# A decoder layer on one core: Relu and square of the up pairs as one pass on VectorE in place of two on ScalarE

## The chip, the cores and the metric
The kernel runs on one core of one Trainium2 chip. The metric is the device time of one execution, in microseconds (us). The engines are TensorE (PE; its weight loads are PEld), VectorE (DVE), ScalarE (ACT), GpSimd (POOL) and SyncE (SP), each with an instruction queue of its own that it works through in order. They wait for each other through semaphores.

## What is computed
One decoder layer on x of 512 x 1024, float32: RMSNorm, one input projection, latent attention and sparse attention, an output projection, then the part that matters here, a squared-ReLU MLP with 4096 hidden columns.

```
h2 = rms_norm(x, ln2_g[l])
x = x + jnp.square(jax.nn.relu(h2 @ w_up[l])) @ w_down[l]
```

## The kernel before
Products are made in float32 accuracy from halves: each factor is split into `hi` (ScalarE copies it, rounded) and `lo` (VectorE subtracts `hi` from the factor), and a product is three matmuls, hi x hi, lo x hi and hi x lo. Weights come in pieces of 128 x 1024 through a ring of three `raw` tiles, are split into a ring of five `w_hi` / `w_lo` tiles, and are used from there. `split_hi(n)` and `split_lo(n)` make the halves of piece n. SyncE loads a piece into `raw` when the tile's last reader has signalled (`lo_done`, for some pieces the subtraction `w_diff` as well).

The hidden columns are 32 chunks of 128; all outputs lie in `a_all` (32 x 512 in the free dimension). The first 4 chunks are done singly (ScalarE's Relu and Square, lines 1286 on, not touched here). The other 28 are done as 14 pairs (PAIRS = 14) with fewer block products, by sums and differences of blocks as in Strassen's method. For pair p:
- TensorE: `sum_products(p)` (24 matmuls of 256 columns from piece A, then 12 called D), `own_products(p + 1)` (24, piece P), `last_products(p)` (24, piece B): 84 a pair. `last_products(p)` waits for `cross_out(p)`. In the last round (p = 13) `job(0)` stands in the place of `own_products`.
- ScalarE: `keep(p)` copies the sum bank to SBUF once A is done.
- VectorE: `cross_out(p)` (line 1848) adds bank and kept sum into the two cross quarters of the pair's output, `first_out(p)` (1856, 1857) updates the kept sum, `diagonal_out(p)` (1864) writes the two diagonal quarters with the sign turned, once B is done. It also makes the weight differences (`diff_of`, `diff_lo`; ScalarE's `diff_hi` between them) and every second pair `row_diffs(i)` (1869, 1870).
- ScalarE then runs, in place on each half of the output (128 x 512), Relu (line 1249, scale 1 on the cross, -1 on the diagonal quarters) and Square (1251). `cross_square(p)` stands behind `keep(p)`, and `diagonal_square(p)` in the next round ahead of `keep(p + 1)`; for the last pair it stands behind `job_hi(3)`.

The down projection is 56 jobs (`JOBS`) of 12 matmuls of 512 columns, 8 steps of 4 and then 8 of 3. Job d needs two splits: `job_hi(d)` on ScalarE (its factor, line 1298, then its weights, 1307) and `job_lo(d)` on VectorE (`factor_lo_of`, 1927, then `weight_lo_of`, 1935; for an m5 job `weight_difference`, 1913, ahead of them). The factors of m1, m2 and m5 are differences that VectorE makes in `factor_of` (1949) from quadrants of the squared `a_all`. Jobs 0 to 3 are m2, m5, m3, m1 of step 0, jobs 4 and 5 are m2 and m5 of step 1. At the seam the order in the queues is written out by hand. VectorE: round 12 ends with `factor_of` m1 and m2 of step 0 and `job_lo(0)`; round 13 is `diagonal_out(12)`, `factor_of("m5", 0)`, `weight_difference(0)`, `factor_lo_of(1)`, `cross_out(13)`, `first_out(13)`; then `weight_lo_of(1)`, `job_lo(2)`, `job_lo(3)`, `diagonal_out(13)`, `factor_of` m1, m2, m5 of step 1, `job_lo(4)`, `job_lo(5)` and so on. ScalarE: `diagonal_square(12)`, `job_hi(1)`, `keep(13)`, `cross_square(13)`, `job_hi(2)`, `job_hi(3)`, `diagonal_square(13)`, `job_hi(4)`.

Of the kernel before, what the change touches and what calls it, by code (L numbers as in the profile page):

```python
# [22 lines left out]
ALU = mybir.AluOpType  # L23
ACT = mybir.ActivationFunctionType
# [37 lines left out]
STARTED = 4  # L62
PAIRS = (N_UP - STARTED) // 2
# [3 lines left out]
JOBS = [(m, i) for i in range(STEPS) for m in (GROUP_A if i < STEPS - 1 else ("m2", "m5", "m1", "m3"))]  # L67
# [257 lines left out]
def build(nc, a, out, known):  # L325
    with ExitStack() as ctx:
# [14 lines left out]
        def signal(name, step=1):  # L341
            return Signal(nc, ctx, name, known, step)
# [119 lines left out]
        def s_halves(d):  # L462
            return s_all[:, d % S_RING, 0, :, :], s_all[:, d % S_RING, 1, :, :]
# [29 lines left out]
        def pair_slots(p):  # L493
            return a_all[:, STARTED + 2 * p:STARTED + 2 * p + 2, :].rearrange("p f (h s) -> p (f h) s", h=2)

        def cross(p):
            return pair_slots(p)[:, 1:3, :]

        def diagonal(p):
            return pair_slots(p)[:, 0::3, :]  # L500

        def pair_sum(p):
            return s_tmp[2 + p % 2]
# [61 lines left out]
        dve_step, x2_done, sq_done, factor_lo = signal("dve_step"), signal("x2_done"), signal("sq_done"), signal("factor_lo")  # L565
        part_in, factor_diff, job_used = signal("part_in"), signal("factor_diff"), signal("job_used")
        rows_kept, g_kept, g_sum, g_hi, g_lo, uv_done = signal("rows_kept"), signal("g_kept"), signal("g_sum"), signal("g_hi"), signal("g_lo"), signal("uv_done")
        weight_diff, pair_kept, pair_out, pair_relu = signal("weight_diff"), signal("pair_kept"), signal("pair_out"), signal("pair_relu")
        y_done = signal("y_done")

        rsqrt_done, pool_step, roped = signal("rsqrt_done"), signal("pool_step"), signal("roped")
# [63 lines left out]
        def pair_banks(p):  # L635

            x_, z_ = (D, S)[p % 2]
            return x_, z_, T[p % 2][:, 0:2 * P]
# [283 lines left out]
        def _(act):  # L922
# [321 lines left out]
                n = PIECE_AT["P", p]  # L1244
                act.activation(d_halves[p % 2][0], raw[:, n % RAW, 0:512], ACT.Copy).then_inc(*hi_done.mark(("d", p)))

            def squared(key, tile, scale):

                act.activation(tile, tile, ACT.Relu, scale=scale).then_inc(*pair_relu.mark(key))
                act.wait_ge(*pair_relu.at(key))  # L1250
                act.activation(tile, tile, ACT.Square).then_inc(*sq_done.mark(key))

            def keep(p):

                if p >= 2:
                    act.wait_ge(*pair_out.at(("diagonal", p - 2)))
                act.wait_ge(*dense_done.at(("A", p)))
                act.activation(pair_sum(p), pair_banks(p)[1].rearrange("p (h s) -> p h s", h=2), ACT.Copy).then_inc(*pair_kept.mark(p))

            def cross_square(p):  # L1260
                act.wait_ge(*pair_out.at(("cross", p)))
                squared(("cross", p), cross(p), 1.0)

            def diagonal_square(p):
                act.wait_ge(*pair_out.at(("diagonal", p)))
                squared(("diagonal", p), diagonal(p), -1.0)

            ln_his(1, [0])
            to_hi(("mix", 1, 0), act_hi[:, 4:8, 0:P], 4, P)
# [11 lines left out]
            for f in range(STARTED):  # L1281
                key = ("up", f)
# [10 lines left out]
            def job_hi(d):  # L1293

                m, i = JOBS[d]
                act.wait_ge(*job_factor_free(d))
                act.wait_ge(*(factor_diff if m in DIFF_OF else uv_done).at(JOBS[d] if m in DIFF_OF else i))
                act.activation(s_halves(d)[0], factor(d), ACT.Copy).then_inc(*factor_hi.mark(JOBS[d]))
                act.wait_ge(*job_slot_free(d))
                if m == "m1":  # L1300
                    act.wait_ge(*dve_step.at(("w_diff", i)))
                    src = w_diff
                else:
                    n = job_piece(d)
                    act.wait_ge(*raw_in[n % RAW].at(n))
                    src = quads(raw[:, n % RAW, :])
                act.activation(job_halves(d)[0], src, ACT.Copy).then_inc(*hi_done.mark(JOBS[d]))  # L1307

            for p in range(PAIRS):
                if p + 2 < PAIRS:  # L1310
                    split_hi(PIECE_AT["P", p + 2])
                if p:
                    diagonal_square(p - 1)
                if p == PAIRS - 1:
                    job_hi(1)
                if p == PAIRS - 2:
                    split_hi(PIECE_AT["B", p + 1])
                keep(p)
                cross_square(p)
                if p + 2 < PAIRS:  # L1320
                    diff_hi(p + 2)
                    split_hi(PIECE_AT["B", p + 1])
                if p + 2 < PAIRS:
                    split_hi(PIECE_AT["A", p + 2])
                if p == PAIRS - 2:
                    job_hi(0)
            job_hi(2)
            job_hi(3)
            diagonal_square(PAIRS - 1)
            for d in range(4, len(JOBS)):  # L1330
                job_hi(d)


# [1 line left out]
        def _(dve):  # L1335
            def split_lo(n):

                width, (hi, lo) = PIECES[n][2], halves_of(n)
                dve.wait_ge(*hi_done.at(n))
                if PIECES[n][0] == "wo":  # L1340
                    for j, gain in enumerate(group_gains(n)):
                        cols = slice(512 * j, 512 * j + 512)
                        ins = dve.scalar_tensor_tensor(lo[:, cols], raw[:, n % RAW, cols], gain,
                                                       hi[:, cols].bitcast(F32), ALU.mult, ALU.subtract)
                else:
                    ins = dve.tensor_tensor(lo[:, 0:width], raw[:, n % RAW, 0:width],  # L1346
                                            hi[:, 0:width].bitcast(F32), ALU.subtract)
                ins.then_inc(*lo_done.mark(n))
# [495 lines left out]
            def cross_out(p):  # L1844
# [2 lines left out]
                dve.wait_ge(*pair_kept.at(p))  # L1847
                dve.tensor_tensor(cross(p), halves(x_)[:, ::-1, :], pair_sum(p), ALU.add).then_inc(*pair_out.mark(("cross", p)))

            def first_out(p):  # L1850

                w_ = pair_banks(p)[2]
                z = pair_sum(p)
                dve.wait_ge(*dense_done.at(("D", p)))
                dve.wait_ge(*pair_out.at(("cross", p)))
                dve.tensor_tensor(z[:, 0, :], z[:, 0, :], w_, ALU.subtract)
                dve.tensor_tensor(z[:, 1, :], z[:, 1, :], w_, ALU.add).then_inc(*pair_out.mark(("first", p)))

            def diagonal_out(p):

                x_, _, _ = pair_banks(p)
                dve.wait_ge(*dense_done.at(("B", p)))
                dve.wait_ge(*pair_out.at(("first", p)))
                dve.tensor_tensor(diagonal(p), halves(x_), pair_sum(p), ALU.add).then_inc(*pair_out.mark(("diagonal", p)))

            def row_diffs(i):

                dve.wait_ge(*sq_done.at(("diagonal", 2 * i - 1) if i else STARTED - 1))
                dve.tensor_tensor(quadrant((0, 1), i), quadrant((0, 0), i), quadrant((0, 1), i), ALU.subtract)
                dve.tensor_tensor(quadrant((1, 0), i), quadrant((1, 0), i), quadrant((1, 1), i), ALU.subtract).then_inc(*uv_done.mark(i))  # L1870

# [88 lines left out]
            for p in range(PAIRS):  # L1960
                if p:
                    diagonal_out(p - 1)
                if p + 2 < PAIRS:
                    split_lo(PIECE_AT["P", p + 2])
                if p == 0:
                    factor_low("G6", 1)
                    factor_low("G6", 0)
                if p == PAIRS - 1:
                    factor_of("m5", 0)
                    weight_difference(0)  # L1970
                    factor_lo_of(1)
                cross_out(p)
                if p + 2 < PAIRS:
                    diff_of(p + 2)
                first_out(p)
                if p + 2 < PAIRS:
                    diff_lo(p + 2)
                if p + 1 < PAIRS:
                    split_lo(PIECE_AT["B", p + 1])
                if p + 2 < PAIRS:  # L1980
                    split_lo(PIECE_AT["A", p + 2])
                if p == 1:
                    row_diffs(0)
                if p and p % 2 == 0:
                    row_diffs(p // 2)
                if p == PAIRS - 2:
                    factor_of("m1", 0)
                    factor_of("m2", 0)
                    job_lo(0)
            weight_lo_of(1)  # L1990
            job_lo(2)
            job_lo(3)
            diagonal_out(PAIRS - 1)
            for m in ("m1", "m2", "m5"):
                factor_of(m, 1)
            for d in range(4, len(JOBS)):
                m, i = JOBS[d]
# [648 lines left out]
```

## Time and profile before
| | us |
|---|---|
| median of 3 runs | 650.25 (649.61 to 651.02) |
| profiled execution, its own time | 649.47 |
| its span, first to last instruction | 647.2 |
| TensorE busy | 637.0 (98%) |
| VectorE busy | 497.7 (77%) |
| ScalarE busy | 395.4 (61%) |
| GpSimd busy | 161.0 (25%) |

The granted clock of TensorE is 1.0 of full speed in every slice. Matmuls are pipelined: one is recorded with 0.28 us (256 columns) or 0.39 us (512), and the next starts 0.12 or 0.23 us behind it; some of their records are missing. So the pace of TensorE is read from start times. Instructions of VectorE and ScalarE overlap a little as well: the next one may start before the recorded end of the one ahead.

### The profile page before, as it was taken

The numbers are of one execution on the slowest core, as the hardware profiler recorded it, in microseconds if no ns is written. First come the engines' busy times: TensorE is split into PE (matmuls) and PEld (weight loads), VectorE is DVE, ScalarE is ACT, GpSimd is POOL, SyncE is SP. The second block draws the span as 40 slices with busy tenths as digits, with TensorE's granted clock in tenths as the row PEclk, the third lists the DMA queues.
The fourth block names the chain that finished last, engine by engine and source line by source line (L and its number), as shares of the span: only waits on it lengthen the run. The fifth ranks groups of instructions, "written<-read, shape, count | busy, mean of one in ns | idle before, by whom it ended". The sixth has DMA issues, their size and how long they took to land.

```text
span 647.2 us, 11797 instructions
## 1 busy us (share of the span) xinstructions
PE 637.0 (98%) x4189; PEld 566.1 (87%) x4189; DVE 497.7 (77%) x915; ACT 395.4 (61%) x784; POOL 161.0 (25%) x229
## 2 busy tenths in 40 slices
PE   8999999999999999998999999999999999999998
PEld 5999888887789888887899999999998888888886
DVE  5665746479887888897786787778768999898675
ACT  6554666467897647556447666757657655565471
POOL 1416755444332201112110111111112221222200
PEclk9999999999999999999999999999999999999999
DMA  8383538998998964896371687887877899999984
GB/s 288 121 310 131 196 129 290 303 305 217 250 269 255 356 205 164 260 268 156 65 188 67 188 236 195 216 217 194 231 177 163 188 250 221 233 237 268 265 246 158
DMA packets 33933, 140.40 MB, mean 217 GB/s; under 512 B 5097, under 2 KB 5481, under 8 KB 32915
## 3 DMA queue, kind: packets, MB, share of 16 engines
q1 hardware_dynamic: 22114, 81.63, 36.2%
q0 software_dynamic: 10208, 34.88, 29.9%
q10 hardware_dynamic: 1552, 23.14, 9.5%
q8 instruction: 34, 0.56, 0.4%
q14 instruction: 25, 0.20, 0.1%
HBM read 137.48 MB, written 65.06 MB: 313 GB/s over the span
## 4 chain that ended last, share of the span: by engine, by line
PE 93%; DVE 3%; ACT 2%; issue 1%; DMA 0%; ACTq 0%; DVEq 0%
PE bank L2052 15%; PE bank L2054 15%; PE bank L2053 15%; PE bank L2469 7%; PE bank L2470 7%; PE bank L2471 7%; PE bank L2072 7%; PE bank L2304 3%; PE bank L2247 2%; PE bank L2286 2%; PE bank L2400 2%; PE bank L2399 2%; PE bank L2401 2%; PE bank L2258 1%; PE bank L2259 1%
## 5 line engine op out<-in xcount | busy, mean ns | idle before, releaser
L841 POOL DMA_DIRECT2D down_sums<-w_down x64 | 49.8, 779 | 235.1 <-PE bank L2471 143.1
L1346 DVE TENSOR_TENSOR w_lo<-raw,w_hi 128x1024 fp32r<-128x1024 f32 (+3 forms) x70 | 80.2, 1158 | 21.8 <-ACT w_hi L938 21.5
L2052 PE MATMUL bank<-w_hi,act_hi 128*128 128x512 f32 (+3 forms) x224 | 89.8, 401 | 2.1 <-DVE act_lo L1360 0.9
L938 ACT ACTIVATE w_hi<-raw 128x1024 fp32r<-128x1024 f32 (+3 forms) x70 | 68.5, 993 | 33.6 <-DMA raw<-w_pairs 22.6
L2053 PE MATMUL bank<-w_lo,act_hi 128*128 128x512 f32 (+3 forms) x224 | 79.8, 356 | 0.0
L2054 PE MATMUL bank<-w_hi,act_lo 128*128 128x512 f32 (+3 forms) x224 | 79.8, 356 | 0.0
L1074 ACT ACTIVATE p_buf<-s_buf,stats 128x128 f32<-128x128 f32 (+3 forms) x96 | 53.8, 561 | 32.4 <-PE bank L2072 18.1
L1307 ACT ACTIVATE w_hi<-raw 128x1024 fp32r<-128x1024 f32 x31 | 32.8, 1059 | 35.9 <-DMA raw<-down_sums 16.9
L2052 PE MATMUL bank<-w_hi,s_all 128*128 128x512 f32 x140 | 54.6, 390 | 0.0
L2053 PE MATMUL bank<-w_lo,s_all 128*128 128x512 f32 x140 | 54.6, 390 | 0.0
L2054 PE MATMUL bank<-w_hi,s_all 128*128 128x512 f32 x140 | 54.5, 390 | 0.0
L2052 PEld LDWEIGHTS bank<-w_hi,act_hi 128*128 128x128 f32 x224 | 42.3, 189 | 10.1 <-issue 2.6
L2053 PEld LDWEIGHTS bank<-w_lo,act_hi 128*128 128x128 f32 x224 | 42.4, 189 | 6.1 <-issue 1.4
L2469 PE MATMUL bank<-g_all,w_hi 128*128 128x256 f32 x168 | 47.7, 284 | 0.0
L2471 PE MATMUL bank<-g_all,w_lo 128*128 128x256 f32 x168 | 47.6, 284 | 0.0
L2471 PE MATMUL bank<-act_hi,w_lo 128*128 128x256 f32 x168 | 47.6, 284 | 0.0
L2469 PE MATMUL bank<-act_hi,w_hi 128*128 128x256 f32 x168 | 47.6, 284 | 0.0
L2470 PE MATMUL bank<-act_lo,w_hi 128*128 128x256 f32 x168 | 47.6, 284 | 0.0
L2470 PE MATMUL bank<-g_all,w_hi 128*128 128x256 f32 x168 | 47.6, 283 | 0.0
L2054 PEld LDWEIGHTS bank<-w_hi,act_lo 128*128 128x128 f32 x224 | 42.2, 188 | 5.4
L1935 DVE TENSOR_TENSOR w_lo<-raw,w_hi 128x1024 fp32r<-128x1024 f32 x31 | 37.8, 1219 | 11.5 <-ACT w_hi L1307 11.4
L2072 PE MATMUL bank<-consts,p_buf 128*128 128x128 f32 x248 | 45.0, 279 | 1.6 <-ACT p_buf L1074 0.8
(313 smaller groups left out, 1830.6 us busy)
## 6 DMA issues: line engine op xcount, KB each, us to landing
down_sums<-w_down ACTq DMA_DIRECT2D x32, 512.0 KB, 6.5
down_sums<-w_down POOLq DMA_DIRECT2D x64, 256.0 KB, 5.6
raw<-down_sums SPq DMA_DIRECT2D x32, 512.0 KB, 5.4
up_sums<-w_pairs POOLq DMA_DIRECT2D x28, 512.0 KB, 10.2
raw<-up_sums SPq DMA_DIRECT2D x28, 512.0 KB, 4.9
raw<-weights SPq DMA_DIRECT2D x26, 512.0 KB, 5.8
up_sums<-w_pairs SPq DMA_DIRECT2D x16, 512.0 KB, 6.5
raw<-w_down SPq DMA_DIRECT2D x16, 512.0 KB, 5.3
```

Source lines behind the costliest of these rows:

```text
L841: pool.dma_start(sums_dram[k, rows_], a["w_down"][SUMS[m][1], step, rows_], accum_op=ALU.add, max_dma_last_dim=4096).then_inc(*sum_added[k ...
L938: ins = act.activation(hi[:, 0:width], raw[:, n % RAW, 0:width], ACT.Copy)
L1074: act.activation(p_buf[:, n % 2, 0:nk], s_buf[:, n % 2, 0:nk], ACT.Exp, scale=-1.0, bias=neg_max[:, m:m + 1], accum_out=den[:, d:d + 1]).t ...
L1346: ins = dve.tensor_tensor(lo[:, 0:width], raw[:, n % RAW, 0:width], hi[:, 0:width].bitcast(F32), ALU.subtract)
L1935: dve.tensor_tensor(lo, src, hi.bitcast(F32), ALU.subtract).then_inc(*lo_done.mark(JOBS[d]))
L2052: pe.matmul(dst, a_h, w_h, start=start, stop=False, skip_group_check=onto)
L2053: pe.matmul(dst, a_h, w_l, start=False, stop=False, skip_group_check=onto)
L2054: return pe.matmul(dst, a_l, w_h, start=False, stop=stop, skip_group_check=onto)
L2072: ins = pe.transpose(bank[0:m, i * step:i * step + k], tile, ident[0:k, 0:k])
L2469: pe.matmul(dst, h[:, k * P:(k + 1) * P], g_h[:, k, :], start=start and k == 0, stop=False, skip_group_check=onto)
L2470: pe.matmul(dst, h[:, k * P:(k + 1) * P], g_l[:, k, :], start=False, stop=False, skip_group_check=onto)
L2471: ins = pe.matmul(dst, l[:, k * P:(k + 1) * P], g_h[:, k, :], start=False, stop=k == KD // 2 - 1, skip_group_check=onto)
```

## The change
Relu and square are no longer two ACTIVATE instructions on ScalarE but one `scalar_tensor_tensor` on VectorE: (t max 0) * t on the cross quarters, (t min 0) * t on the diagonal ones, whose sign is turned. It is still in place and still 128 x 512. `keep`, `job_hi` and the others on ScalarE stay in their order without the squares; the new passes stand in VectorE's queue.

```diff
-            def squared(key, tile, scale):
-
-                act.activation(tile, tile, ACT.Relu, scale=scale).then_inc(*pair_relu.mark(key))
-                act.wait_ge(*pair_relu.at(key))
-                act.activation(tile, tile, ACT.Square).then_inc(*sq_done.mark(key))
-
...
-            def cross_square(p):
-                act.wait_ge(*pair_out.at(("cross", p)))
-                squared(("cross", p), cross(p), 1.0)
-
-            def diagonal_square(p):
-                act.wait_ge(*pair_out.at(("diagonal", p)))
-                squared(("diagonal", p), diagonal(p), -1.0)
...
             for p in range(PAIRS):
                 if p + 2 < PAIRS:
                     split_hi(PIECE_AT["P", p + 2])
-                if p:
-                    diagonal_square(p - 1)
                 if p == PAIRS - 1:
                     job_hi(1)
...
                 keep(p)
-                cross_square(p)
...
             job_hi(2)
-            job_hi(3)
-            diagonal_square(PAIRS - 1)
-            for d in range(4, len(JOBS)):
+            for d in range(3, len(JOBS)):
                 job_hi(d)
...
+            def squared(key, tile, op):
+
+                dve.wait_ge(*pair_out.at(key))
+                dve.scalar_tensor_tensor(tile, tile, 0.0, tile, op, ALU.mult).then_inc(*pair_squared.mark(key))
+
...
             def row_diffs(i):
 
-                dve.wait_ge(*sq_done.at(("diagonal", 2 * i - 1) if i else STARTED - 1))
+                if i:
+                    dve.wait_ge(*pair_squared.at(("diagonal", 2 * i - 1)))
+                else:
+                    dve.wait_ge(*sq_done.at(STARTED - 1))
...
                     diagonal_out(p - 1)
                 if p + 2 < PAIRS:
                     split_lo(PIECE_AT["P", p + 2])
+                if p:
+                    squared(("diagonal", p - 1), diagonal(p - 1), ALU.min)
...
                 first_out(p)
+                squared(("cross", p), cross(p), ALU.max)
                 if p + 2 < PAIRS:
                     diff_lo(p + 2)
...
             job_lo(3)
             diagonal_out(PAIRS - 1)
+            squared(("diagonal", PAIRS - 1), diagonal(PAIRS - 1), ALU.min)
             for m in ("m1", "m2", "m5"):
                 factor_of(m, 1)
```

## Rows read from the trace of the kernel before

**Rows 1.** The page, busy time of the engines (share of the span, instructions).
```profile
PE 637.0 (98%) x4189; PEld 566.1 (87%) x4189; DVE 497.7 (77%) x915; ACT 395.4 (61%) x784; POOL 161.0 (25%) x229
```

**Rows 2.** The page, the chain that ended last, by engine.
```profile
PE 93%; DVE 3%; ACT 2%; issue 1%; DMA 0%; ACTq 0%; DVEq 0%
```

**Rows 3.** Windows over pairs and first jobs: length, then busy us of each engine.
```profile
362.00:472.00 110.00, 110.00 (x919) 110.00 (x919) 83.62 (x113) 72.69 (x101) 17.12 (x22) 1.00 0.79 211
505.12:516.21 11.09, 11.09 (x50) 8.94 (x48) 11.09 (x15) 6.44 (x8) 2.33 (x3) 1.00 0.85 214
```

**Rows 4.** Timeline of TensorE, pair 13 and jobs: start, duration, instruction.
```profile
491.41 0.28 PE L2469 MATMUL bank<-act_hi,w_hi 128*128 128x256 f32 x1
...
494.28 0.40 PE L2052 MATMUL bank<-w_hi,s_all 128*128 128x512 f32 x1
...
502.47 0.39 PE L2052 MATMUL bank<-w_hi,s_all 128*128 128x512 f32 x1
...
504.96 0.39 PE L2054 MATMUL bank<-w_hi,s_all 128*128 128x512 f32 x1
505.26 0.47 PE L2052 MATMUL bank<-act_hi,s_all 128*128 128x512 f32 x1
...
516.35 0.47 PE L2052 MATMUL bank<-w_hi,s_all 128*128 128x512 f32 x1
```

**Rows 5.** Timeline of VectorE, pairs 11 to 13 and jobs; brackets: idle before, releaser.
```profile
467.95 0.69 DVE L1848 TENSOR_TENSOR a_all<-bank,spare 128x512 f32<-128x512 f32 x1 [1.13 <-ACT spare L1258]
...
470.52 0.69 DVE L1839 TENSOR_TENSOR d<-raw,d 128x512 fp32r<-128x512 f32 x1 [0.62 <-ACT d L1245]
...
486.10 0.69 DVE L1864 TENSOR_TENSOR a_all<-bank,spare 128x512 f32<-128x512 f32 x1
486.81 0.69 DVE L1949 TENSOR_TENSOR spare<-a_all,spare 128x512 f32<-128x512 f32 x1
...
490.10 0.69 DVE L1848 TENSOR_TENSOR a_all<-bank,spare 128x512 f32<-128x512 f32 x1 [0.74 <-ACT spare L1258]
...
491.56 1.22 DVE L1935 TENSOR_TENSOR w_lo<-raw,w_hi 128x1024 fp32r<-128x1024 f32 x1
...
493.62 1.23 DVE L1935 TENSOR_TENSOR w_lo<-raw,w_hi 128x1024 fp32r<-128x1024 f32 x1 [0.24 <-ACT w_hi L1307]
...
498.01 0.69 DVE L1949 TENSOR_TENSOR s_tmp<-spare,a_all 128x512 f32<-128x512 f32 x1
498.62 0.69 DVE L1949 TENSOR_TENSOR s_tmp<-a_all,spare 128x512 f32<-128x512 f32 x1
499.46 0.69 DVE L1927 TENSOR_TENSOR s_all<-s_tmp,s_all 128x512 fp32r<-128x512 f32 x1 [0.15 <-ACT s_all L1298]
500.41 1.23 DVE L1935 TENSOR_TENSOR w_lo<-raw,w_hi 128x1024 fp32r<-128x1024 f32 x1 [0.26 <-ACT w_hi L1307]
...
503.90 1.22 DVE L1935 TENSOR_TENSOR act_lo<-raw,act_hi 128x1024 fp32r<-128x1024 f32 x1
```

**Rows 6.** Groups of ScalarE by line and form: busy us, mean ns, idle before.
```profile
L1249 ACT ACTIVATE a_all<-a_all 128x512 f32<-128x512 f32 x28 | 17.6, 628 | 19.4 <-DVE a_all L1848 12.4 <-DVE a_all L1864 6.9
```

**Rows 7.** Groups of VectorE by line and form, the instructions nearest to the new one.
```profile
L1377 DVE SCALAR_TENSOR_TENSOR ln_row<-x,stats,gain_ln 128x512 f32<-128x512 f32 x4 | 3.0, 744 | 0.0
...
L1377 DVE SCALAR_TENSOR_TENSOR ln_row<-x,stats,gain_ln 128x1024 f32<-128x1024 f32 x2 | 2.6, 1278 | 1.9 <-POOL stats L895 1.9
...
L1816 DVE SCALAR_TENSOR_TENSOR g_tmp<-bank,n_q 128x512 f32<-128x512 f32 x1 | 0.7, 681 | 0.0
...
L1797 DVE TENSOR_SCALAR mix_row<-o_nsa,stats 128x512 f32<-128x512 f32 x1 | 0.5, 485 | 0.7 <-POOL stats L754 0.7
```

**Rows 8.** Timeline of ScalarE, `job_hi(1)`'s factor, `keep(13)`, `job_hi(4)`'s factor.
```profile
488.02 0.62 ACT L1298 ACTIVATE s_all<-spare 128x512 fp32r<-128x512 f32 x1
...
489.49 0.57 ACT L1258 ACTIVATE spare<-bank 128x512 f32<-128x512 f32 x1
...
498.80 0.63 ACT L1298 ACTIVATE s_all<-s_tmp 128x512 fp32r<-128x512 f32 x1 [0.28 <-DVE s_tmp L1949]
```

More of the change, by code:

```diff
@@ L567, in build @@
         rows_kept, g_kept, g_sum, g_hi, g_lo, uv_done = signal("rows_kept"), signal("g_kept"), signal("g_sum"), signal("g_hi"), signal("g_lo"), signal("uv_done")
-        weight_diff, pair_kept, pair_out, pair_relu = signal("weight_diff"), signal("pair_kept"), signal("pair_out"), signal("pair_relu")
+        weight_diff, pair_kept, pair_out, pair_squared = signal("weight_diff"), signal("pair_kept"), signal("pair_out"), signal("pair_squared")
         y_done = signal("y_done")
```

## Prediction
> **What bounds the kernel now.** I read the shares of busy time first [rows 1]: TensorE is busy for 637.0 of 647.2 us, VectorE for 77% of the span. The chain of waits [rows 2] puts 93% of the time that decides the end on TensorE. So a change on VectorE and ScalarE can only matter where it makes TensorE wait. The windows [rows 3] show where VectorE has room. In the pairs (362 to 472 us) TensorE is busy without a gap, while VectorE works 83.62 and ScalarE 72.69 of 110 us. From 505.12 to 516.21 us, in the first jobs of the down projection, VectorE is busy for all of the 11.09 us.
>
> The timeline of TensorE [rows 4] shows what that means. The 24 products of `last_products(13)` run from 491.41 to 494.28, so one of 256 columns takes 0.12 us and a pair of 84 takes 10.08 us. Jobs 1 to 3 (36 products of 512 columns) run from 494.28 to 502.47, 2.73 us a job. Job 4 then should hand over to job 5 at 502.47 + 2.72 = 505.19, but its first product starts at 505.26. VectorE's `weight_lo_of(5)` starts at 503.90 [rows 5] and takes 1.22 us, so it ends at 505.12, and TensorE starts 0.14 us behind it. TensorE has run into VectorE there. The last product of job 4 starts at 504.96, so the distance is 0.30 us where 2.73 / 12 = 0.23 is usual. Job 9, four jobs on, starts at 516.35, again later than products alone would bring it (505.26 + 4 x 2.73 = 516.18). Between the two VectorE has no idle time. The reader is to see that VectorE, off the path by the shares, sets the end in this one place: what is put into its queue ahead of 505 us and isn't hidden by an idle stretch comes out at the end one for one.
>
> **ScalarE's side.** The change takes 56 passes off ScalarE. The 28 Relus mean 628 ns [rows 6], and I count their Squares alike. ScalarE isn't on the path, and it waits 19.4 us just before these Relus, so its relief is worth only what it lets VectorE do sooner.
>
> **Cost of one fused pass.** The trace has no `scalar_tensor_tensor` of this very shape. Nearest [rows 7]: with an immediate scalar, 128x512, one input in PSUM, it takes 681 ns; with a per-partition scalar and all inputs in SBUF, 744 ns. Below, as the low bound, stands the TENSOR_SCALAR of 128x512 with 485 ns. I take 0.68 us, since the immediate is what the new pass has too. What matters in a full queue is the distance from start to start: 498.01 to 498.62 is 0.61 us for a tensor_tensor of 0.69 us that doesn't wait for the one before it [rows 5]; 486.10 to 486.81, where the second waits for the first one's output, is 0.71. One fused pass is 0.61 us.
>
> A rule of the Trainium skill speaks against this. Rows 7 show 744 ns for 512 and 1278 ns for 1024 elements, both with two f32 inputs in SBUF: 1.04 ns an element, as a plain tensor_tensor costs (0.69 us for 512, 1.22 for 1024) [rows 5]. The Trainium skill's Vector Engine (DVE) Microarchitecture Reference, section "Points that are easy to get wrong", says that such an instruction with two SBUF sources that aren't bf16 runs at half the throughput. By that rule a pass would cost some half a microsecond more and the forecast would be 654.1 instead of 652.0; this trace does not bear it out.
>
> **In the pairs.** Each gets two fused passes, 1.2 us. VectorE's 83.62 us over 110 / 10.08 = 10.9 pairs are 7.7 us a pair. They become 8.9, and in the pairs that also hold `row_diffs` (1.2 us more every second pair, so 0.6 above the mean) 9.5, under the 10.08 us of TensorE. The places are right as well. The pass on the diagonal falls ahead of `cross_out`, where VectorE idles for `keep` (1.13 us in pair 11), and `keep` waits for TensorE. The pass on the cross products falls ahead of `diff_lo`, where it idles 0.62 us because `diff_hi` stood behind `cross_square` on ScalarE [rows 5]; now `diff_hi` comes sooner and the pass fills the hole. Cost in the pairs: nothing, with some 0.6 us of a heavy pair as cover. Without it, each heavy pair would cost what it runs over.
>
> **At the seam to the jobs.** Four passes now stand in VectorE's queue between 479 and 499 us. I follow the shift of its instructions [rows 5] and ScalarE's [rows 8].
> - Cross, pair 12: +0.61. `diagonal_out(12)` moves from 486.10 to 486.71. It was waiting for nothing, so all of it counts.
> - Diagonal, pair 12: the pass waits for `diagonal_out` (0.71) and adds 0.61. `factor_of(m5, 0)` moves from 486.81 to 488.03. On ScalarE `job_hi(1)` stood behind the two passes on this diagonal and began at 488.02, 0.52 us after its input was ready (486.81 + 0.69). Now it waits for VectorE alone and begins at 488.03 + 0.69 + 0.10 = 488.82 (the 0.10 from `job_hi(4)`: its input is made from 498.01 to 498.70, it begins at 498.80). `keep(13)` follows it at its old distance, 489.49 + 0.80 = 490.29, and so `cross_out(13)` moves from 490.10 to 490.90. The shift of 1.22 has shrunk to 0.80, since part of the idle 0.74 us took it up. `cross_out(13)` ends at 491.59; with the 0.14 us seen above TensorE starts `last_products(13)` at 491.73 and not 491.41: a first stall of 0.3 us.
> - Cross, pair 13: +0.61, shift 1.41. `weight_lo_of(1)` starts at 492.97 and ends at 494.19, just ahead of TensorE's need at 494.28 + 0.3.
> - The idle 0.24 us ahead of 493.62 (waiting for ScalarE's `w_hi`) goes, as ScalarE is ahead there without `cross_square(13)`: shift 1.17, for `diagonal_out(13)` too.
> - Diagonal, pair 13: +0.61, shift 1.78. The idle 0.15 and 0.26 us ahead of 499.46 and 500.41 stay: they are ScalarE's answer to `factor_of(m2, 1)` at 498.01, which itself moves.
>
> `weight_lo_of(4)` ends at 500.41 + 1.78 + 1.23 = 503.42, TensorE gets job 4 at 503.56 and not 502.47 (its lead was 0.83 us), and job 5 at 505.26 + 1.78 = 507.04. From there VectorE was full and stays full, so job 9 comes 1.78 later too. Behind it VectorE gets idle time again, but TensorE has none to give back: the shift stays to the end. Where I could read the small waits either way the sum came out between 1.68 and 1.78; I take 1.7. The loads of `raw` that SyncE issues behind `lo_done` and `w_diff` move with the shift, and nothing else stands behind them.
>
> The profiled execution took 649.47 us, 2.3 more than its span; with 1.7 it would be 651.2. The runs have their median at 650.25, so the forecast is 650.25 + 1.7 = 652.0 us, slower by 0.26%. A change under 0.2% (1.3 us) can't be told from none here.
>
> **The rivals.**
> - *ScalarE's relief hides it (not slower).* The place is the wait of `cross_out(13)` for `keep(13)`. If ScalarE's `keep` came early enough, the 0.5 us left of that wait goes, and if the answers at 499.46 and 500.41 shortened too (0.15 + 0.26), the shift is 1.7 - 0.9 = 0.8, time 651.0. For it: ScalarE waited 19.4 us over its Relus. Against: `keep(13)` is issued behind `job_hi(1)`, which waits for VectorE's own output. It decides from 0.4 us gained. Chance 0.18.
> - *The pass is shorter.* Both inputs are one tile. If it ran like the TENSOR_SCALAR (485 ns), four passes save 0.2 us each: shift 0.9, time 651.1, again within 0.2%. Against: no row has such a rate for this instruction. It decides from 0.1 us a pass. Chance 0.08.
> - *The pass runs at half the rate.* Each costs another 512 elements, 1278 - 744 = 534 ns; four make 2.1 us more at the seam, 3.8 in all, time 654.1. A heavy pair is then 9.5 + 1.1 = 10.6 us of VectorE, over TensorE's 10.08, but a light one is 9.4, and the pairs hold. Against: the 1278 ns. Chance 0.05.
> - *Faster.* At best TensorE's two small gaps at 505.26 and 516.35 go, 0.2 us together; that is not 0.2%. I leave 0.03 for what I don't see.
>
> **How the numbers follow.** Forecast 0.66, then 0.18, 0.08, 0.05 and 0.03. The low end, 650.6, holds most of the hidden case and of the short pass with half a microsecond for the runs; the high end, 653.1, takes the forecast with passes of 744 ns (0.06 more each, 652.2) and a further loss of 0.9; the half rate is left out. Slower by over 0.2%: 0.66 + 0.05, less a little for a shift that comes out just under 1.3 us: 0.69. Within: 0.28. Faster: 0.03.
>
> **What would show it.** Right: no wait of TensorE between 360 and 485 us; the fused passes at 0.68 us; `cross_out(13)` near 490.9; job 4 starting near 503.5, job 5 near 507.0, job 9 near 518.1, each right behind a VectorE `weight_lo_of`. Wrong: a VectorE that still idles ahead of job 4 other than for ScalarE's answers, passes of under 0.6 or over 1 us, or gaps of TensorE inside the pairs.

## The result and the profile after

| | kernel before | changed kernel |
|---|---|---|
| median of the runs, us | 650.1 (649.26 to 652.66, 22 runs) | 652.33 (651.12 to 655.36, 22 runs) |
| ratio | 1 | 1.0033, 95% interval 1.0024 to 1.0042 |
| profiled execution, its span | 647.2 | 649.1 |

The change makes the kernel 0.33% slower, 2.2 us by the medians; the interval lies clear of 1. The page of the changed kernel answers to [rows 1, 2]: VectorE has 14.7 us more, ScalarE 32.4 less, TensorE is as busy as before, but its share of the chain falls from 93 to 88% and VectorE's rises from 3 to 6%.

```profile
span 649.1 us, 11769 instructions
PE 637.8 (98%) x4189; PEld 566.3 (87%) x4189; DVE 512.4 (79%) x943; ACT 363.0 (56%) x728; POOL 160.8 (25%) x229
...
PE 88%; DVE 6%; ACT 3%; issue 2%; DMA 0%; ACTq 0%; DVEq 0%
```

The window over the pairs answers to [rows 3]. VectorE works 94.63 us of 110 and not 83.62, 8.7 us a pair of 10.08, and TensorE still has no gap.

```profile
362.00:472.00 110.00, 110.00 (x919) 110.00 (x918) 94.63 (x134) 47.16 (x56) 17.13 (x22) 1.00 0.81 211
```

By its group on VectorE, the new pass takes 685 ns, where 0.68 us was assumed:

```profile
L1834 DVE SCALAR_TENSOR_TENSOR a_all<-a_all 128x512 f32<-128x512 f32 x28 | 19.2, 685 | 0.1
```

The timeline of TensorE answers to [rows 4]. Of the products shown here, three now name VectorE as what they waited for: the first of `last_products(13)` at 491.84, of job 4 at 503.66 and of job 5 at 507.14. The first of job 9, at 518.23, has the small gap of before.

```profile
491.11 0.39 PE L2047 MATMUL bank<-w_hi,s_all 128*128 128x512 f32 x1
491.84 0.39 PE L2462 MATMUL bank<-act_hi,w_hi 128*128 128x256 f32 x1 [0.34 <-DVE a_all L1829]
...
502.78 0.39 PE L2047 MATMUL bank<-w_hi,s_all 128*128 128x512 f32 x1
503.66 0.47 PE L2045 MATMUL bank<-w_hi,s_all 128*128 128x512 f32 x1 [0.49 <-DVE w_lo L1924]
503.97 0.39 PE L2046 MATMUL bank<-w_lo,s_all 128*128 128x512 f32 x1
...
507.14 0.47 PE L2045 MATMUL bank<-act_hi,s_all 128*128 128x512 f32 x1 [0.47 <-DVE act_lo L1924]
...
517.92 0.39 PE L2047 MATMUL bank<-w_hi,s_all 128*128 128x512 f32 x1
518.23 0.47 PE L2045 MATMUL bank<-w_hi,s_all 128*128 128x512 f32 x1
```

From 491.11 to 491.84 are 0.73 us where 0.23 is usual, a loss of 0.50; at 503.66 the distance from the product ahead is 0.88 us, a loss of 0.65; at 507.14 it is 0.86, a loss of 0.63.

The timeline of VectorE at the seam, against [rows 5], shows who was late (line 1834 is the fused pass, 1850 `diagonal_out`, 1829 `cross_out`, 1924 `weight_lo_of`):

```profile
479.42 0.68 DVE L1834 SCALAR_TENSOR_TENSOR a_all<-a_all 128x512 f32<-128x512 f32 x1
...
483.08 0.69 DVE L1938 TENSOR_TENSOR spare<-spare,a_all 128x512 f32<-128x512 f32 x1
484.81 0.69 DVE L1916 TENSOR_TENSOR s_all<-spare,s_all 128x512 fp32r<-128x512 f32 x1 [1.03 <-ACT s_all L1284]
...
486.90 0.68 DVE L1850 TENSOR_TENSOR a_all<-bank,spare 128x512 f32<-128x512 f32 x1
487.62 0.69 DVE L1834 SCALAR_TENSOR_TENSOR a_all<-a_all 128x512 f32<-128x512 f32 x1
488.23 0.68 DVE L1938 TENSOR_TENSOR spare<-a_all,spare 128x512 f32<-128x512 f32 x1
...
491.10 0.69 DVE L1829 TENSOR_TENSOR a_all<-bank,spare 128x512 f32<-128x512 f32 x1 [0.45 <-ACT spare L1252]
...
492.56 0.68 DVE L1834 SCALAR_TENSOR_TENSOR a_all<-a_all 128x512 f32<-128x512 f32 x1
493.16 1.22 DVE L1924 TENSOR_TENSOR w_lo<-raw,w_hi 128x1024 fp32r<-128x1024 f32 x1
494.30 0.68 DVE L1916 TENSOR_TENSOR s_all<-a_all,s_all 128x512 fp32r<-128x512 f32 x1
494.90 1.22 DVE L1924 TENSOR_TENSOR w_lo<-raw,w_hi 128x1024 fp32r<-128x1024 f32 x1
...
498.49 0.69 DVE L1834 SCALAR_TENSOR_TENSOR a_all<-a_all 128x512 f32<-128x512 f32 x1
...
502.29 1.23 DVE L1924 TENSOR_TENSOR w_lo<-raw,w_hi 128x1024 fp32r<-128x1024 f32 x1 [0.26 <-ACT w_hi L1293]
...
505.77 1.22 DVE L1924 TENSOR_TENSOR act_lo<-raw,act_hi 128x1024 fp32r<-128x1024 f32 x1
```

`weight_lo_of(4)` starts at 502.29 and not 500.41, `weight_lo_of(5)` at 505.77 and not 503.90. Each is the last thing that TensorE's job waits for. The timeline of ScalarE, against [rows 8], shows `job_hi(1)`'s factor and `keep(13)`:

```profile
489.00 0.63 ACT L1284 ACTIVATE s_all<-spare 128x512 fp32r<-128x512 f32 x1 [3.28 <-DVE spare L1938]
...
490.49 0.57 ACT L1252 ACTIVATE spare<-bank 128x512 f32<-128x512 f32 x1
```

### The profile page after: what moved, and what is told of

Same layout as the page of the kernel before. It is cut to its first block, busy times and chain, and to the rows that moved or that the text cites. A ratio compares the mean times of both kernels' runs of the same rounds, so it can differ in the third digit from the quotient of the medians.

```text
span 649.1 us, 11769 instructions
## 1 busy us (share of the span) xinstructions
PE 637.8 (98%) x4189; PEld 566.3 (87%) x4189; DVE 512.4 (79%) x943; ACT 363.0 (56%) x728; POOL 160.8 (25%) x229
## 4 chain that ended last, share of the span: by engine, by line
PE 88%; DVE 6%; ACT 3%; issue 2%; DMA 0%; ACTq 0%; DVEq 0%
PE bank L2045 15%; PE bank L2047 14%; PE bank L2046 14%; PE bank L2065 7%; PE bank L2462 7%; PE bank L2464 7%; PE bank L2463 7%; PE bank L2297 3%; PE bank L2240 2%; PE bank L2279 2%; PE bank L2394 2%; PE bank L2393 2%; PE bank L2392 2%; PE bank L2251 1%; PE bank L2252 1%
```

## The experiments

One stretch of the profiles needs care. The first product of the pairs starts at 350.3 us in some executions and as late as 352.8 in others, of kernels that are alike up to there. `spread` and `spread_again` below are one and the same kernel and have 350.54 and 352.35, so it isn't the edits. What it is stays open; it adds scatter to spans and runs. So beside the runs I give for each profile the time from that product to the end of the span. For the two kernels it is 647.2 - 350.37 = 296.83 and 649.1 - 350.30 = 298.80, 1.97 us more. A span is given to 0.1 us, so a difference of two of these times can be off by 0.1 us; where that matters, I read start times instead. These are the first products, before and after:

```profile
350.37 0.34 PE L2469 MATMUL bank<-g_all,w_hi 128*128 128x256 f32 x1
```

```profile
350.30 0.33 PE L2462 MATMUL bank<-g_all,w_hi 128*128 128x256 f32 x1
```

| kernel | median us | median of before beside it | ratio (95% interval) | first product of the pairs to the end, us |
|---|---|---|---|---|
| before | | | | 296.83 |
| changed | 652.33 | 650.1 | 1.0033 (1.0024 to 1.0042) | 298.80 |
| seam_only | 652.36 | 651.0 | 1.0025 (1.001 to 1.0041) | 298.52 |
| pairs_only | 650.41 | 651.0 | 0.999 (0.9973 to 1.0008) | 296.89 |
| last_only | 651.81 | 651.0 | 1.0009 (0.9993 to 1.0025) | 297.52 |
| cross_only | 651.0 | 650.66 | 1.0006 (0.9988 to 1.0023) | 298.42 |
| seam_more | 653.32 | 650.82 | 1.0041 (1.0026 to 1.0057) | 300.04 |
| one_more | 652.53 | 650.82 | 1.0029 (1.0015 to 1.0043) | 299.18 |
| three_more | 654.58 | 650.82 | 1.0053 (1.0034 to 1.0072) | 301.69 |
| rows_late | 651.07 | 650.66 | 1.0008 (0.9987 to 1.0029) | 296.68 |
| spread | 651.16 | 651.0 | 1.0019 (0.9994 to 1.0044) | 296.46 |
| spread_again | 650.79 | 650.66 | 1.0008 (0.999 to 1.0026) | 296.45 |
| late_scalar | 650.04 | 650.82 | 0.9989 (0.997 to 1.0008) | 296.44 |

**Which of the 28 passes cost: seam_only and pairs_only.** A function chooses the engine of each square. The rest keep the order of the kernel before or of the changed one.

```diff
+def on_vector(kind, p):
+    return p >= PAIRS - 2      # seam_only; pairs_only has p < PAIRS - 2
...
                 keep(p)
+                act_squared("cross", p)     # Relu and Square on ScalarE unless on_vector
```

> Only the four squares of pairs 12 and 13 are fused passes on VectorE; those of pairs 0 to 11 are Relu and Square on ScalarE as in the kernel before. Seam theory (VectorE's full queue between 479 and 505 us is what costs): as slow as the full change, 1.9 us over the kernel before on the span, 652.0; job 4 of TensorE near 503.6 us, job 5 near 507.1. Load theory (the fused passes cost wherever they stand, so by their number): 4 of 28, 0.3 us over the kernel before, 650.4.

> The 24 squares of pairs 0 to 11 are fused passes on VectorE, the four of pairs 12 and 13 are on ScalarE as in the kernel before. Seam theory: the time of the kernel before, 650.1, span 647.2, TensorE without a gap in the pairs, jobs 5 and 9 at 505.3 and 516.4. Load theory: 24 of 28 of the loss, 1.9 us over, 652.0.

The four passes at the seam alone bring 1.69 of the 1.97 us, with TensorE's first products of jobs 4 and 5 held up as in the changed kernel (`seam_only`):

```profile
504.26 0.47 PE L2073 MATMUL bank<-w_hi,s_all 128*128 128x512 f32 x1 [0.50 <-DVE w_lo L1952]
...
507.73 0.47 PE L2073 MATMUL bank<-act_hi,s_all 128*128 128x512 f32 x1 [0.51 <-DVE act_lo L1952]
```

The 24 in the pairs bring 0.06 us, and the runs show no loss. The load theory wanted 0.3 us for the first and 1.9 us for the second, and the runs exclude both: `seam_only` is at least 1.001, 0.65 us, over the kernel before, and `pairs_only` at most 1.0008, 0.5 us. It is out. The two parts make 1.75 us and not 1.97; the rest arises only when all 28 have moved (the part on the prediction shows where). (In seam_only and pairs_only the pairs begin at 351.18 and 352.81 us, so their times on the clock stand 0.8 and 2.4 us later than what was expected; the distances are what count.)

**One pass alone: last_only and cross_only.**

```diff
-    return p >= PAIRS - 2
+    return (kind, p) == ("diagonal", PAIRS - 1)    # last_only
+    return (kind, p) == ("cross", PAIRS - 2)       # cross_only
```

> Only the square of the diagonal of pair 13 is a fused pass on VectorE, ahead of the factors of step 1; the rest is as in the kernel before. Seam theory: VectorE has no idle time behind it that could take it up, so its whole 0.6 us reaches the end: 650.7, job 5 near 505.9. Load theory: 1 of 28, under 0.1 us. ScalarE is freed of two passes there, so if its relief were worth anything at this place it would come out under 0.6.

> Only the cross square of pair 12 is a fused pass on VectorE, in round 12; the rest as in the kernel before. Seam theory: everything behind it on VectorE moves by 0.6 us, ScalarE's answers and diagonal_square(12) with it, since they wait for VectorE's own output; so 0.5 to 0.7 us more from the first product of the pairs to the end (297.4), 650.7. Rival: the idle 0.74 us ahead of cross_out(13) takes it up, and there is no loss: 296.8, 650.1.

In `last_only` job 5 starts at 505.88, 0.61 us later than before (the pairs begin at 350.38), and the way to the end is 0.69 us longer: one pass, one for one. ScalarE's two passes less at this place bring nothing. The interval of the runs, 0.9993 to 1.0025, holds both this and nothing, so here only the profile speaks. In `cross_only` job 5 starts at 505.87, again 0.6 us later than before, and the idle time ahead of `cross_out(13)` is still 0.74 us:

```profile
490.70 0.69 DVE L1851 TENSOR_TENSOR a_all<-bank,spare 128x512 f32<-128x512 f32 x1 [0.74 <-ACT spare L1259]
```

So that idle time does not take the pass up: everything behind it moved by 0.6 us, `keep(13)` too. In the queue of ScalarE that stands behind `diagonal_square(12)` and `job_hi(1)`, and both wait for VectorE's own output. That far the expectation held. But the whole came to 1.59 us more and not 0.6. The further 1 us arises at job 9, which starts 12.03 us behind job 5 where the kernel before has 11.09. The timeline of ScalarE in `cross_only` shows a load that came late:

```profile
510.75 1.06 ACT L1310 ACTIVATE w_hi<-raw 128x1024 fp32r<-128x1024 f32 x1 [3.70 <-DMA raw<-w_down]
```

In the kernel before the same instruction starts at 508.84, 5.39 us after the SyncE issue at 503.45; here it is 6.69 us after the issue at 504.06. The load was 1.3 us slower and VectorE idled 0.84 us for it. One execution doesn't tell whether this belongs to the edit. For the same load the changed kernel has 4.66 us, `seam_only` 4.37 and `one_more` 6.14, so it scatters widely. The median of the runs (1.0006) speaks for an accident of that execution, but their interval reaches to 1.0023, 1.5 us.

**Two more passes at the seam: seam_more.**

```diff
             squared(("diagonal", PAIRS - 1), diagonal(PAIRS - 1), ALU.min)
+            again("cross", PAIRS - 1)      # the same form: t * 1 max t, in place
+            again("cross", PAIRS - 2)
```

> The full change with two further passes of the same form and size on VectorE, right behind the square of the last diagonal; each leaves its squared tile as it is (t * 1 max t). Seam theory: 0.6 us each, one for one, so 1.2 to 1.3 over the full change: 3.5 over the kernel before, 653.6, job 5 near 508.4. Rival (VectorE is only just late there, so a part of it is taken up elsewhere): under 0.6 over the full change.

From the first product of the pairs to the end there are 300.04 - 298.80 = 1.24 us more than in the changed kernel, two passes at 0.62. Nearly all of it is in the wait of job 4, which grew from 0.49 to 1.70 us:

```profile
507.14 0.47 PE L2055 MATMUL bank<-w_hi,s_all 128*128 128x512 f32 x1 [1.70 <-DVE w_lo L1932]
```

By the runs it is 2.5 us over the kernel before, where 3.5 were expected, in an interval of 1.7 to 3.7. The slope of one for one rests on the profile.

**How much cover the pairs have: one_more and three_more.**

```diff
                 squared(("cross", p), cross(p), ALU.max)
+                if 2 <= p < PAIRS - 2:
+                    again("cross", p - 1)
...
+                    again("diagonal", p - 1)      # three_more only
+                    again("cross", p)             # three_more only
```

> The full change with one further pass of the same form and size on VectorE in each of rounds 2 to 11 of the pairs (10 passes, the tile stays as it is). Seam theory: VectorE has 1.2 us left in a mean pair and 0.6 in a heavy one, so they are hidden: the time of the full change, 652.3, no gap in the pairs. Load theory: 10 passes more on 28, 0.8 us over it, 653.1.

> The full change with three further passes on VectorE in each of rounds 2 to 11 (30 passes, tiles stay as they are). This takes the cover away: a mean pair is 8.9 + 1.8 = 10.7 us of VectorE against TensorE's 10.08, so it falls behind by 0.6 us a pair, 6 us over ten pairs, less the lead that VectorE has at the start. Seam theory: 1 to 6 us over the full change, 653 to 658, with gaps of TensorE in the later pairs or a later seam. If the pairs had more cover than I worked out: 652.3 still.

With ten passes more VectorE works 100.04 of the 110 us and TensorE still has no gap in the pairs; from their first product to job 0 it is 138.29 us, as in all kernels so far (within 0.01). The runs are at 1.0029 and the changed kernel's at 1.0033. The 0.38 us that its profile has over the changed kernel lie at job 9 (a load again, ScalarE waits 3.14 us for it and VectorE 0.29 for ScalarE). With thirty passes more the cover is gone. The windows over the pairs, first `one_more`, then `three_more`:

```profile
362.00:472.00 110.00, 110.00 (x919) 110.00 (x918) 100.04 (x145) 48.11 (x57) 17.12 (x22) 1.00 0.79 211
```

```profile
362.00:472.00 110.00, 109.08 (x903) 108.27 (x902) 105.53 (x155) 44.26 (x53) 17.12 (x22) 1.00 0.76 205
```

Job 0 comes 140.28 us behind the first product, 2 us late, and `last_products(13)` waits 1.1 us for `cross_out(13)`, where the changed kernel has 0.34. That makes the 2.89 us that `three_more` takes over the changed kernel:

```profile
PE bank L2476 <- DVE a_all L1829: 1.1, 1, 1.1
PE bank L2476 <- DVE a_all L1856: 0.7, 2, 0.5
```

Line 1856 is `diagonal_out`, so in the pairs TensorE now waits for a free bank. So the pairs forgive one further pass a pair and not three. The expectation had wanted VectorE to fall behind by 6 us over the ten pairs, less its lead at the start; of that 2 us reached TensorE there. How the rest divides between that lead and too high an estimate of the load stays open.

**The same work at another place: rows_late, spread and late_scalar.** Pairs 12 and 13 are read only by the row differences of step 7, and these only by the factors of step 7. So nothing needs their squares at the seam.

```diff
-                if m == "m2" and i == 2:
+                if m == "m3" and i in (2, 3, 4, 5):        # spread: one square a step, on VectorE
+                    squared(...)                           # late_scalar: on ScalarE, behind its job_hi
+                if m == "m2" and i == STEPS - 2:           # all three; rows_late has only this
                     row_diffs(STEPS - 1)
```

> The kernel before with one thing changed: the row differences of step 7 (two passes of VectorE, 1.2 us) move from step 2 to step 6 of the jobs. Seam theory: the gap of TensorE at job 9 goes and the one at job 5 stays. From the first product of the pairs to the end it is then 296.7 us instead of 296.8; 650.1 by the runs, no difference that they can show. If VectorE were not what TensorE runs into at job 9, the gap of 0.31 us there would stay.

> All 28 squares are fused passes on VectorE, but the four of pairs 12 and 13 stand behind the m3 jobs of steps 2 to 5, one each, and the row differences of step 7 move from step 2 to step 6. Nothing needs them sooner. Seam theory: the loss of the full change is gone, since they meet a VectorE that has idle time again; with the row differences out of step 2 the gap of TensorE at job 9 goes too, so 649.9 to 650.2. Load theory: 652.3 as the full change, since it has as many passes on VectorE.

> The kernel with all 28 fused passes and the last four behind the jobs, once more, since its runs scattered from 649.3 to 656.9. Seam theory: its median is that of the kernel before within 0.5 us, 649.8 to 650.8, and from the first product of the pairs to the end it has 296.5 us again. If this order had a loss that its profile did not show, it would again be over 651.

> Squares of pairs 0 to 11 fused on VectorE; those of pairs 12 and 13 are Relu and Square on ScalarE, but behind its m3 jobs of steps 2 to 5, and the row differences of step 7 in step 6. At the seam neither engine has a square. Seam theory: cross_out(13) comes up to 0.5 us sooner than in the kernel before, so the small gaps of TensorE at jobs 5 and 9 go: 649.9 to 650.1, at best 0.2 us under the kernel before, which can hardly be measured. Load theory: 651.9.

`rows_late` loses the gap at job 9 and keeps that at job 5 (505.31). Its way to the end is 0.15 us shorter than before, 296.68; by start times job 10 comes 0.18 us sooner behind the first product (519.03 - 350.42 = 168.61, before 519.16 - 350.37 = 168.79). `spread` has as many passes on VectorE as the changed kernel and in both profiles no gap at any job; 296.46 and 296.45 are 2.35 us less than the changed kernel and 0.37 less than the kernel before. `late_scalar` is the same with 296.44, though its `cross_out(13)` comes only 0.12 us sooner than before and not up to 0.5 (491.97 - 352.36 against 490.10 - 350.37).

The expectation of `spread` said that the four passes meet a VectorE with idle time. They don't: from 516 to 549 us VectorE is busy for all of the 33.00 us, in `spread` and in the kernel before. What counts is its pace. In `spread` `weight_lo_of(13)` starts at 524.34 and `weight_lo_of(17)` at 534.83, so four jobs with one of the squares take VectorE 10.49 us, and TensorE needs 10.9 for four jobs. VectorE still gains on it there.

```profile
524.34 1.22 DVE L1924 TENSOR_TENSOR act_lo<-raw,act_hi 128x1024 fp32r<-128x1024 f32 x1
...
527.82 0.69 DVE L1834 SCALAR_TENSOR_TENSOR a_all<-a_all 128x512 f32<-128x512 f32 x1
...
534.83 1.22 DVE L1924 TENSOR_TENSOR w_lo<-raw,w_hi 128x1024 fp32r<-128x1024 f32 x1
```

By the runs `spread` was expected within 650.2 and came out at 651.16, up to 656.9, with the kernel before at 651.0 beside it; its repetition is at 650.79 beside 650.66. The first interval, 0.9994 to 1.0044, holds both 1 and the changed kernel's 1.0033, so it decides nothing; the second, 0.999 to 1.0026, holds 1 and not 1.0033. So the loss of the changed kernel is gone. That this order is 0.4 us or 0.06% under the kernel before stands in the profiles alone; the runs can't tell the two apart.

## Why the prediction was right

The forecast was 652.0 us, slower by 0.26%, and the runs gave 652.33 and 0.33%. The mechanism was the one forecast, and the size came out a little over it. Point by point:

- **The pass.** 681 ns were taken from [rows 7], 685 measured, and 0.61 us from start to start. The rivals of a short and of a half-rate pass fall with it. The Trainium skill's Vector Engine (DVE) Microarchitecture Reference, section "Points that are easy to get wrong", says that such an instruction with two SBUF sources that aren't bf16 runs at half the throughput. The trace does not agree: both inputs here are f32 in SBUF, and the 685 ns are what a plain tensor_tensor of the size takes, 0.69 us.
- **The pairs.** Right: hidden. `pairs_only` shows it by itself, and `one_more` and `three_more` show the size of the cover. I had 0.6 us in a heavy pair as cover; one pass more (0.61 us) was still free. The load grew by 1.0 us a pair and not 1.2.
- **The seam.** The forecast said shifts of VectorE of 0.61, 0.80, 1.41, 1.17 and 1.78 us. They can be read from start times, each counted from the first product of the pairs (which puts 0.07 us on the differences of the changed kernel's times on the clock):

| start of | forecast | `seam_only` | changed |
|---|---|---|---|
| `diagonal_out(12)` | 0.61 | 0.59 | 0.87 |
| `cross_out(13)` | 0.80 | 0.79 | 1.07 |
| `weight_lo_of(1)` | 1.41 | 1.40 | 1.67 |
| `weight_lo_of(2)` | 1.17 | 1.07 | 1.35 |
| `weight_lo_of(4)` | 1.78 | 1.67 | 1.95 |

  With only the four passes moved, the working holds within 0.02 us up to `weight_lo_of(1)` and is 0.1 too high behind it, since the wait ahead of `weight_lo_of(2)` took up 0.33 us and not 0.24. In the changed kernel 0.28 us more is there from the start: ScalarE's answer to `factor_of(m2, 0)`. VectorE ended that at 483.77 and `job_hi(0)` began at 484.14, 0.37 us later; before it was 0.09, and VectorE's idle time ahead of `factor_lo_of(0)` grew from 0.76 to 1.03.
- **A slip in the working.** The forecast let the wait for `keep(13)` take up 0.42 of its 0.74 us and then spoke of 0.5 us left, where that leaves 0.32. Measured are 0.45, because `factor_lo_of(1)`, too, no longer waits for ScalarE: it follows the start of `weight_difference(0)` by 1.13 us (488.83 to 489.96) and not 1.25 (487.42 to 488.67). It touches only the price of the rival that ScalarE's relief hides the cost.
- **The stops.** `last_products(13)` was forecast to start 0.32 us late and started 0.50 late (491.84 - 491.41 + 0.07); jobs 4 and 5 were forecast at 503.56 and 507.04 and came at 503.66 and 507.14, job 9 at 518.23. The jobs start 0.14 or 0.15 us behind the end of a VectorE `weight_lo_of`, as assumed; `last_products(13)` starts 0.05 us behind `cross_out(13)`, where I had put the same 0.14. The distance to the kernel before stayed the same to the end (1.88 us on the clock at jobs 5 and 9, so 1.95 with the start of the pairs taken out, and 1.97 on the whole).
- **The size.** 1.97 us in the profile against 1.7 forecast. `seam_only` has 1.69, and the 0.28 us that the changed kernel has over it are that late answer of ScalarE, which the forecast did not foresee. This is read from the traces; no run changes that answer alone. That 1.69 meets 1.7 so closely is partly luck, since the step at `weight_lo_of(2)` was 0.1 us off and 1.7 lies low in what the working gave. The rest of the medians' 2.2 us lies within the scatter of the runs.
- **ScalarE's relief** was the rival on the other side. A part of it came, and the forecast had counted it: in the kernel before `job_hi(1)` began 0.52 us after its input was ready, held by `diagonal_square(12)`; in the changed kernel it is 0.09, so that `keep(13)` moved by 1.07 us where its input's maker, `factor_of(m5, 0)`, moved by 1.49. More could not come: by the timeline of ScalarE above, `job_hi(1)` has waited 3.28 us for VectorE when it starts, and `keep(13)` stands behind it.
- **The rival "faster"** priced TensorE's two small gaps at 0.2 us together. `spread` and `late_scalar` have neither and are 0.37 to 0.39 us shorter than the kernel before, so they cost about twice that. It is still not 0.2%.

## What to carry to other kernels

A queue that is 77% busy can still be the one that the bottleneck runs into for a few microseconds; look for places where a start of the bottleneck stands right behind an end on the other engine, and treat every instruction ahead of it as on the path until an idle stretch that doesn't depend on the same engine stands between them. Moving work to an engine with room on average pays or costs by where it lands: here, by the profiles, 24 passes were free and 4 cost 1.7 us, and the same 4 a little later were free again. The later place need not have idle time; it is enough that the queue with the extra work still goes faster than the bottleneck (10.49 against 10.9 us for four jobs). Ask what reads the result: work whose reader is far off should not stand in a queue at a seam between stages.

## What was not expected of the hardware

- A stop of TensorE costs more than its wait. In the kernel before, job 5 starts 0.07 us after it could, but its second product follows 0.31 us behind the first, where 0.23 is usual. `rows_late` removes one such stop, whose wait was 0.08 us, and gains 0.18 us by the start of job 10. After the longer waits of the changed kernel the 0.31 us is the same (503.66 to 503.97).
- ScalarE answered VectorE's `factor_of(m2, 0)` after 0.37 us in the changed kernel, `spread` (both times), `late_scalar`, `seam_more`, `one_more` and `three_more`, and after 0.09 or 0.10 in the kernel before, `rows_late`, `seam_only`, `pairs_only`, `last_only` and `cross_only`. In the first group ScalarE has been idle for 5.6 to 6.2 us, but so it has in `seam_only` and `cross_only` with 5.94. What tells the groups apart is that in the first no square stands on ScalarE in round 12 of the pairs, neither the diagonal of pair 11 nor the cross of pair 12. Why that should cost 0.27 us stays open. The two timelines of ScalarE, changed kernel and `seam_only`, where VectorE's input ended at 483.77 and at 484.64:

```profile
484.14 0.63 ACT L1284 ACTIVATE s_all<-spare 128x512 fp32r<-128x512 f32 x1 [6.22 <-DVE spare L1938]
```

```profile
484.74 0.63 ACT L1301 ACTIVATE s_all<-spare 128x512 fp32r<-128x512 f32 x1 [5.94 <-DVE spare L1966]
```
